# The feed-forward layer's gate and up projection with the weights as the stationary operand, and a down projection that starts before the last gate group is out

## What is computed

```python
h = rmsnorm(x, g_pre_ffn[l]) * (1.0 + sc_f) + sh_f
f = (jax.nn.silu(h @ w_gate[l]) * (h @ w_up[l])) @ w_down[l]
x = x + gt_f * rmsnorm(f, g_post_ffn[l])
```

## Time and profile before

| | |
|---|---|
| median of 3 runs | 2523.65 us (2519.93 to 2524.54) |
| the profiled execution, device time | 2519.91 us |
| its span, first to last instruction | 2518.1 us |
| mean granted TensorE clock | 0.978 of full speed (full is 2.4 GHz) |
| TensorE busy with matmuls | 2365.1 us, 94% of the span |
| VectorE, ScalarE, GpSimd busy | 66%, 45%, 4% |
| read from HBM | 596.74 MB, 238 GB/s over the span |

### The profile page before, as it was taken

One profiled execution on the slowest core, in us unless ns is written; L12 is line 12 of the kernel. 1 busy time (PEld: TensorE's weight loads), 2 busy tenths in 40 slices (PEclk: granted clock), 3 DMA queues, 4 the chain that ended last, 5 costly groups with the idle time before them and its releaser, 6 DMA issues.

```text
span 2518.1 us, 27287 instructions
## 1 busy us (share of the span) xinstructions
PE 2365.1 (94%) x10764; PEld 1956.9 (78%) x10764; DVE 1669.7 (66%) x1786; ACT 1133.4 (45%) x1473; POOL 98.1 (4%) x62
## 2 busy tenths in 40 slices
PE   1399999979999999899969999999999999999997
PEld 1288788868888888788858888888888888888886
DVE  6898778978888888655554555556556555555565
ACT  2244666554444444444454433443445544444453
POOL 1000000001111111200000000000000001000000
PEclk9599999989999999999989999999999999999999
DMA  8898668958899999755534655555655657655553
GB/s 324 342 353 321 210 223 311 344 207 325 325 327 326 331 325 328 281 203 196 188 130 162 210 182 189 181 180 177 209 199 198 207 197 247 212 186 198 184 188 113
DMA packets 246612, 600.51 MB, mean 238 GB/s; under 512 B 11800, under 2 KB 12120, under 8 KB 239968
## 3 DMA queue, kind: packets, MB, share of 16 engines
q1 hardware_dynamic: 243520, 589.43, 67.1%
q0 software_dynamic: 2976, 9.49, 1.2%
HBM read 596.74 MB, written 2.13 MB: 238 GB/s over the span
## 4 chain that ended last, share of the span: by engine, by line
PE 90%; DVE 6%; ACT 1%; DMA 1%; issue 1%; DVEq 0%; SPq 0%; ACTq 0%
PE PS L1151 19%; PE PS L1152 19%; PE PS L1157 19%; PE PS L1123 10%; PE PS L1126 10%; PE PS L1132 10%; DVE BIAS L1562 4%; DMA RAW<-in_w_ada 1%; DVE LO L1544 1%; PE PS L1477 1%; PE PS L1247 0%; PE PS L1222 0%; PE PS L1423 0%; PE PS L1140 0%; PE PS L1194 0%
## 5 line engine op out<-in xcount | busy, mean ns | idle before, releaser
L1544 DVE TENSOR_TENSOR LO<-RAW,HI 128x1024 fp32r<-128x1024 f32 x808 | 1014.4, 1260 | 740.1 <-ACT HI L657 738.9
L657 ACT ACTIVATE HI<-RAW 128x1024 fp32r<-128x1024 f32 x808 | 854.3, 1059 | 1230.0 <-PE PS L1157 732.4
L1151 PE MATMUL PS<-HI,XH 128*128 128x512 f32 x2176 | 863.3, 397 | 3.1 <-DVE XL L1693 3.1
L1152 PE MATMUL PS<-HI,XL 128*128 128x512 f32 x2176 | 849.2, 390 | 0.0
L1157 PE MATMUL PS<-LO,XH 128*128 128x512 f32 x2176 | 583.4, 390 | 0.0
L1151 PEld LDWEIGHTS PS<-HI,XH 128*128 128x128 f32 x2176 | 409.8, 188 | 92.1 <-ACT HI L657 4.3
L1157 PEld LDWEIGHTS PS<-LO,XH 128*128 128x128 f32 x2176 | 409.0, 188 | 86.1
L1152 PEld LDWEIGHTS PS<-HI,XL 128*128 128x128 f32 x2176 | 409.7, 188 | 82.5 <-issue 1.0
L1562 DVE SCALAR_TENSOR_TENSOR BIAS<-RAW,CACT,BIAS 128x1024 f32<-128x1024 f32 x270 | 346.3, 1283 | 19.0 <-DMA RAW<-in_w_ada 11.4
L1123 PE MATMUL PS<-HI,XH 128*128 128x512 f32 x1056 | 327.7, 392 | 4.1 <-ACT HI L657 4.0
L1126 PE MATMUL PS<-HI,XL 128*128 128x512 f32 x1056 | 326.0, 390 | 0.0
(11 more groups left out here) (283 smaller groups left out, 1016.1 us busy)
## 6 DMA issues: line engine op xcount, KB each, us to landing
RAW<-in_w_in SPq DMA_DIRECT2D x208, 1024.0 KB, 5.0
RAW<-in_w_ada SPq DMA_DIRECT2D x144, 1024.0 KB, 5.7
RAW<-in_w_gate SPq DMA_DIRECT2D x88, 512.0 KB, 4.6
RAW<-in_w_up SPq DMA_DIRECT2D x88, 512.0 KB, 5.7
RAW<-in_w_down SPq DMA_DIRECT2D x44, 1024.0 KB, 4.8
RAW<-in_w_out SPq DMA_DIRECT2D x32, 1024.0 KB, 5.2
RAW<-in_w_proj_b SPq DMA_DIRECT2D x16, 1024.0 KB, 5.1
RAW<-in_w_proj_a SPq DMA_DIRECT2D x16, 1024.0 KB, 5.1
```

What stands on the lines that cost most here:

```text
L657: act.activation(HI[:, (it["half"] + hf) % HLS, :], RAW[:, it["slot"], hf * 1024:(hf + 1) * 1024], ACT.Copy).then_inc(s.hi_ready, 1)
L1151: pe.matmul(PS[:, bank + u, :], XH[:, 2 * n + kk, rows], hi, start=start and kk == 0, stop=False)
L1152: pe.matmul(PS[:, bank + u, :], XL[:, 2 * n + kk, rows], hi, start=False, stop=False)
L1544: dve.tensor_tensor(LO[:, slot, :], RAW[:, it["slot"], hf * 1024:(hf + 1) * 1024], HI[:, slot, :].bitcast(F32), ALU.subtract).then_inc(s.l ...
```

## The change

The matmuls of gate and up swap their operands. `turned_products` uses as stationary operand 128 of the 1024 weight columns of a half and as moving operand all 256 positions of XH or XL: 8 blocks of columns, each with HI by XH and HI by XL, then 8 with LO by XH, 24 matmuls in all. Block j goes to bank `4q + j // 2`, columns 0 to 255 or 256 to 511, so the gate columns take banks 4q and 4q + 1, the up columns 4q + 2 and 4q + 3. Only the first matmul into a bank carries `start`. The results now have the inner features on the partitions: `gated` writes its product straight to `FT`, and `f_turn`, `f_chunks` and the semaphore `f_t` are gone; what waited for `group_out` waits for `f_ready`.

At the end of the layer the first down tile is worked off in two parts: both its weight halves for positions 128 to 255 (banks 4 to 7), then, after a wait for `f_ready` 11, both for positions 0 to 127 (banks 0 to 3, where group 10 lay). `group_evac(10)` and `gated(10)` move behind the first down halves on ACT and DVE, `root_table()` behind the eighth. `products` gets an argument `rows`, which positions it works on.

```diff
@@ -259,7 +259,7 @@
 
     add("ada", [("A",)] * 32, 1)
     add("first", first_body(), 1)
-    add("ffn", ffn_body(), 1, groups=11, per_slot_dmas=2)
+    add("ffn", ffn_body(), 1, per_slot_dmas=2)
     add("down", [("W", k) for k in range(4)], NKF // 4)
     add("second", [("W", g, k) for g in range(GROUPS_2) for k in range(0, NK, 4)], 1, groups=GROUPS_2)
     assert plan.ada == ADA_GROUPS
@@ -661,17 +661,9 @@
 
                 q, sec = g % 2, secs["ffn"]
                 act.wait_ge(s.half_used, sec.half(0, 16 * (g + 1)))
-                wait(act, s.f_t, g - 1)
-                act.activation(FG[:, q, :].rearrange("p (u n) -> p u n", u=NT),
-                               PS[:, 4 * q:4 * q + 4:2, :], ACT.Silu).then_inc(s.f_silu, 1)
-
-            def f_chunks(g):
-
-                q = g % 2
-                act.wait_ge(s.f_t, g + 1)
-                act.activation(FT[:, 4 * g:4 * g + 4, :],
-                               PS[:, 4 * q:4 * q + 2, :].rearrange("p b (k t) -> p (b k) t", t=S),
-                               ACT.Copy).then_inc(s.group_out, 1)
+                wait(act, s.f_ready, g - 1)
+                act.activation(FG[:, q, :].rearrange("p (b n) -> p b n", b=2), PS[:, 4 * q:4 * q + 2, :], ACT.Silu)\
+                   .then_inc(s.f_silu, 1)
 
             def stream(name):
                 sec = secs[name]
@@ -679,13 +671,21 @@
                 def emit(i):
                     first = isinstance(i, int) and i == 0
                     for it in sec.items:
-                        k = 4 * i + it["what"][0]
-
-                        act.wait_ge(s.half_used, sec.half0 if first else sec.half(i, it["half"]) - 6)
-                        act.activation(XH[:, it["what"][0], :], FT[:, bass.ds(k, 1), :].rearrange("p a t -> p (a t)"),
+                        kk = it["what"][0]
+                        k = 4 * i + kk
+                        if first:
+                            act.wait_ge(s.half_used, secs["ffn"].half(0, 160 + kk + 1))
+                        else:
+                            act.wait_ge(s.half_used, sec.half(i, it["half"]) - 6)
+                            act.wait_ge(s.f_ready, 11)
+                        act.activation(XH[:, kk, :], FT[:, bass.ds(k, 1), :].rearrange("p a t -> p (a t)"),
                                        ACT.Copy).then_inc(s.xs_hi, 1)
                         for hf in range(2):
+                            if first and kk == 1 and hf == 1:
+                                group_evac(10)
                             hi_half(sec, i, it, hf)
+                        if first and kk == 3:
+                            root_table()
                 looped(act, sec, emit)
 
             def squares(src_of, junk):
@@ -966,11 +966,7 @@
                     at = h % 16
                     if g and at == 3:
                         group_evac(g - 1)
-                    if g and at == 13:
-                        f_chunks(g - 1)
-            group_evac(10)
-            f_chunks(10)
-            root_table()
+            act.wait_ge(s.f_ready, 1)
             stream("down")
             post(3, secs["down"])
             row_norm(4, 2)
@@ -1112,34 +1108,34 @@
 
         @block.tensor
         def _(pe):
-            def products(ready, slot, slot_k, bank_of, first, last):
+            def products(ready, slot, slot_k, bank_of, first, last, rows=range(NT)):
 
                 pe.wait_ge(s.hi_ready, ready)
-                for u in range(NT):
-                    rows = slice(u * P, (u + 1) * P)
-                    xh, xl = XH[:, slot_k, rows], XL[:, slot_k, rows]
+                for u in rows:
+                    xh, xl = (v[:, slot_k, u * P:(u + 1) * P] for v in (XH, XL))
+                    for x in (xh, xl):
+                        for cc in range(2):
+                            pe.matmul(PS[:, bank_of(u, cc), :], x, HI[:, slot, cc * 512:(cc + 1) * 512],
+                                      start=first and x is xh, stop=False)
+                pe.wait_ge(s.lo_ready, ready)
+                for u in rows:
                     for cc in range(2):
-                        cols, o = slice(cc * 512, (cc + 1) * 512), PS[:, bank_of(u, cc), :]
-                        pe.matmul(o, xh, HI[:, slot, cols], start=first, stop=False)
-                    for cc in range(2):
-                        cols, o = slice(cc * 512, (cc + 1) * 512), PS[:, bank_of(u, cc), :]
-                        pe.matmul(o, xl, HI[:, slot, cols], start=False, stop=False)
+                        m = pe.matmul(PS[:, bank_of(u, cc), :], XH[:, slot_k, u * P:(u + 1) * P],
+                                      LO[:, slot, cc * 512:(cc + 1) * 512], start=False, stop=last)
+                return m
+
+            def turned_products(ready, slot, k, bank, first, last):
+
+                pe.wait_ge(s.hi_ready, ready)
+                for j in range(8):
+                    w, o = HI[:, slot, j * P:(j + 1) * P], PS[:, bank + j // 2, j % 2 * S:j % 2 * S + S]
+                    pe.matmul(o, w, XH[:, k, :], start=first and j % 2 == 0, stop=False, skip_group_check=True)
+                    pe.matmul(o, w, XL[:, k, :], start=False, stop=False, skip_group_check=True)
                 pe.wait_ge(s.lo_ready, ready)
-                for u in range(NT):
-                    rows = slice(u * P, (u + 1) * P)
-                    for cc in range(2):
-                        cols, o = slice(cc * 512, (cc + 1) * 512), PS[:, bank_of(u, cc), :]
-                        m = pe.matmul(o, XH[:, slot_k, rows], LO[:, slot, cols], start=False, stop=last)
+                for j in range(8):
+                    m = pe.matmul(PS[:, bank + j // 2, j % 2 * S:j % 2 * S + S], LO[:, slot, j * P:(j + 1) * P], XH[:, k, :],
+                                  start=False, stop=last, skip_group_check=True)
                 m.then_inc(s.half_used, 1)
-
-            def f_turn(g):
-                q = g % 2
-                pe.wait_ge(s.f_ready, g + 1)
-                for kk in range(4):
-                    for u in range(NT):
-                        m = pe.transpose(PS[:, 4 * q + kk // 2, (kk % 2) * S + u * P:(kk % 2) * S + (u + 1) * P],
-                                         FG[:, q, u * 512 + kk * P:u * 512 + (kk + 1) * P], IDENT[:])
-                m.then_inc(s.f_t, 1)
 
             def narrow(sec, h, n, bank, start, stop):
 
@@ -1165,11 +1161,20 @@
                     first = isinstance(i, int) and i == 0
                     for it in sec.items:
                         k = it["what"][0]
+                        pe.wait_ge(s.xs_lo, 4 * i + k + 1)
+                        if k == 0 and first:
+                            for rows in ((1,), (0,)):
+                                if rows == (0,):
+                                    pe.wait_ge(s.f_ready, 11)
+                                for hf in range(2):
+                                    m = products(sec.half(i, hf) + 1, hf, 0, lambda u, cc: 4 * u + 2 * hf + cc, True, False, rows)
+                                    if rows == (0,):
+                                        m.then_inc(s.half_used, 1)
+                            continue
                         for hf in range(2):
                             h = it["half"] + hf
-                            if hf == 0:
-                                pe.wait_ge(s.xs_lo, 4 * i + k + 1)
-                            products(sec.half(i, h) + 1, h % HLS, k, lambda u, cc: 4 * u + 2 * hf + cc, k == 0 and first, k == 3 and last_pass)
+                            products(sec.half(i, h) + 1, h % HLS, k, lambda u, cc: 4 * u + 2 * hf + cc, False, k == 3 and last_pass)\
+                                .then_inc(s.half_used, 1)
                 emit(0)
                 with pe.Fori(1, sec.n_iter - 1) as i:
                     emit(i)
@@ -1390,20 +1395,16 @@
                 for hf in range(2):
                     h = it["half"] + hf
                     if k + hf == 0:
-                        wait(pe, s.group_out, g - 1)
+                        wait(pe, s.f_ready, g - 1)
                     if h < 16 and h % 2 == 0:
                         pe.wait_ge(s.x_ready, TURNED[0] + h // 2 + 1)
-                    products(sec.half(0, h) + 1, h % HLS, k + hf, lambda u, cc: 4 * q + 2 * u + cc, k + hf == 0, k + hf == NK - 1)
+                    turned_products(sec.half(0, h) + 1, h % HLS, k + hf, 4 * q, k + hf == 0, k + hf == NK - 1)
                     if h in (1, 3, 5, 7):
                         turn_pair(0, 4 + h // 2)
-                    if k + hf == 9 and g:
-                        f_turn(g - 1)
                     if g == 10 and k + hf == 13:
                         pe.wait_ge(s.mod_in, 32)
                         pe.wait_ge(s.f_ready, 10)
                         pe.transpose(PS[:, 6, 0:64], MODT[:, :], IDENT[0:64, 0:64]).then_inc(s.mod_t, 1)
-            f_turn(10)
-            pe.wait_ge(s.group_out, 11)
             pe.wait_ge(s.mod_ready, 3)
             stream("down")
             pe.wait_ge(s.post_done, 4)
```

(9 more changed lines are left out.)

## The result

The changed kernel takes 2533.64 us (2531.73 to 2534.58, 6 runs), the kernel before 2522.46 us (2519.93 to 2525.92, 6 runs beside them). The ratio is 1.0043 with a 95% interval of 1.003 to 1.0056: 11.2 us slower. The profiled execution took 2531.75 us, its span is 2529.9 us at a mean clock of 0.979 (before: 2519.91, 2518.1, 0.978).

What follows compares the result with a forecast made beforehand. TensorE's own stream was taken as the bound; +4.9 (matmuls), -9.0 (transposes) and -7.65 (hole before down) gave 2508.2 us for the profiled execution, 2512 us against the median, with an 8-in-10 range of 2502 to 2537.

Steps and rivals of the forecast that it cites:

- What bounds the kernel: Whole kernel: TensorE's own stream sets the time, PE busy 94% of the span, 100 of 100 us inside gate and up.
- Part 1: Gate and up: 24 matmuls of 256 columns at 114.5 ns make a half 2.748 us, not 2.72; +4.9 us.
- half of the 10: Gate and up: of 10 ns lost while float32r columns stream, 256 columns lose 5, plus 3 per matmul; 114.7 ns.
- The prediction's own sign of being wrong: Gate and up: matmul pace outside 113 to 116 ns, or TensorE waiting there for `HI`, `LO` or weights.
- the toll: Gate and up: the 13.4 ns are a fixed loss per matmul, 120.1 ns at 256 columns; +28.6 us, chance 0.24.
- Part 2: Inside gate and up: ten groups' transposes, 0.9 us each, leave TensorE's stream; -9.0 us.
- Part 3: Step before down: early down matmuls shrink 9.35 us lost to a 1.7 us wait for VectorE; -7.65 us.
- The first rival: Gate and up: twice as many matmuls pay 13.4 ns each, +28.6 us in place of +4.9; 2535.6 us, chance 0.24.
- the second: Gate and up: weight loads decide the pace, 111 ns per matmul, -9.9 us; 2497 us, chance 0.12.
- The third: Step before down: VectorE held again or clock falling to 1.2 GHz, -2.1 in place of -7.65; 2517.5 us, chance 0.10.
- The fourth: Gate and up: no float32r pace at 256 columns, 217 ns per matmul, +437 us; 2944 us, chance 0.04.

Runs made afterwards that it cites:

- The chains: Kernels with the whole computation left out, running only 96 matmuls of each form back to back; float32r paces 226.7 ns at 512 columns, 120.0 at 256.
- The experiment with the old step: Changed kernel, but group 10 evacuated and the table loaded before the first down tile, which is worked off whole again: 2538.95 us, ratio 1.0061.

## Why the prediction was wrong

**What bounds the kernel: right.** TensorE's stream set the time in gate and up, nothing waited for `HI`, `LO` or weights, and the loads' own row, full for 100 of 100 us now, did not decide: the pace is 120.0 and a load's floor 111.7. The chains bear out that floor, which the prediction had read as 111 in the earlier trace rows.

**Part 1, the matmuls: wrong, and this is nearly the whole miss.** The step that failed is "I take half of the 10 for half the columns". The bound above it, "if the 13.4 ns are a fixed toll per matmul, 106.7 + 13.4 = 120.1 ns", is what happened: 120.0. So the term was +28.2 us (176 x 0.16) and not +4.9, 23.3 us more, of the 23.6 by which the profiled execution (2531.75) missed the forecast for it (2508.2). The prediction's own sign of being wrong, a pace outside 113 to 116 ns, was met. The evidence that led there was plain float32 at 256 columns, which streams as long as 512 columns of float32r and loses 10 ns less. The observation stands (215.8 beside 226.7 ns in the chains; by their count it is one of two records that a float32 matmul leaves, so the "two clocks per column" of the prediction are those of a record, not of a matmul), but it compares two types and says nothing of two widths. A comparison of types at one stream length can't divide a loss between columns and matmuls; only the same type at two widths can, and the trace held none. With one width known, the toll was the simpler reading of the earlier trace rows, and at 0.24 it was given too little. Even so it holds for this form and not as a law: with 64 stationary columns the loss does grow with the width, 6.7 ns at 256 and 16.7 at 512. That 2533.64 lies inside the range for 8 in 10, up to 2537, comes of stretching the range to this rival; the forecast itself had the wrong sign.

**Part 2, the transposes: right.** Gate and up grew by 18.85 us; with +28.2 for the matmuls, -9.35 is left, beside the -9.0 of 10 x 0.9. In the trace of before a half with the transposes behind it takes 3.515 us and the next one 2.82 to 2.83, against 2.720: 0.90 us for each.

**Part 3, the hole: right in mechanism, a little small.** -8.7 in place of -7.65. The wait came out at 0.65 us, not 1.7: VectorE was through with the modulation at 1057.67, 2.0 us ahead of 1059.65, where down can start (before 1037.79 and 1039.17, 1.4 us), about half of that because its addition began earlier, about half because it took 3.29 us and not 3.61; and its queue took 1057.70 to 1063.01, 5.31 us, not 5.72, because neighbouring operations overlap a little. The clock stayed at 1.00. The 0.17 us that were lost just behind the wait are not in these 0.65. The experiment with the old step shows the same from the other side: about 5 us of the 8.7 belong to the early start; the rest went with the last group's transposes, the chunks behind them and part of the wait.

**The sum.** With the measured terms it is 28.2 - 9.35 - 8.7 = 10.15; with 0.2 inside down, 1.63 ahead (not put down to the change) and -0.2 behind, that is the 11.8 of the profiled executions, and the medians say 11.2. The first rival's own number, 2535.6, is 2 us off: the -1.05 of part 3, and a median of before that came out 1.2 us lower over six runs. The measured pace, 120.0, also lies beyond the 117.3 ns per matmul above which the rival had the change come out slower.

**The other rivals.** The loads' 111.7 ns show only from some 224 columns down, so the second falls. The third (the hole stays in part) falls with 0.65 us. The fourth falls too: with 24 matmuls and 24 loads, 164 of the 176 halves took 2.88 us.

## What to carry to other kernels

Before swapping the operands of a product, count its matmuls: which side moves sets how many there are (256 positions moving make twice as many as 512 weight columns), and every one loses something beside its columns, 13.3 ns here for float32r with 128 stationary columns at 512, 384, 320 and 256, against 2.5 ns for bfloat16. A loss known at one width is to be priced as fixed per instruction too, and another type's row doesn't decide it; a chain of 96 matmuls of the very form does. And take a change apart: this one joined a loss of 19 us to a gain of 8.7, and the gain alone, put on the kernel before, gave 2515.41 us, below both.

## What the runs showed of the hardware beside this

- Plain float32 leaves two records for each matmul, 215.8 ns each at 256 moving columns and 429.2 at 512, 111.7 at 128. So a float32 matmul of 512 columns costs 858 ns, 3.8 times a float32r one.
- Fewer stationary columns can cost pace: 226.7 ns with 128, 233.3 with 120, 230.0 with 96 or 64, 231.7 with 32, all float32r with 512 moving.
- Two forms in turn are slower than their own paces add up to: bfloat16 beside float32r at 256 columns pays 15 ns a pair.
- VectorE's addition of 32 columns took 3.29 us beside POOL's reduction over the partitions, as the 3.61 in the earlier trace rows. Beside the seven other reductions of either trace a `LO` of 128x1024 took 4.0 to 5.6 us instead of 1.22. The Trainium skill, SBUF — State Buffer, section SBUF: two separate sides, calls the port pair of VectorE and GpSimd an exclusive lock, held for the whole instruction; it concerns a VectorE instruction with two SBUF inputs when GpSimd's reads SBUF. By that page the addition would end behind POOL's instruction. In the trace it ended at 1057.45 and POOL's row at 1058.99, and the next VectorE operations ran at 0.18, 0.42 and 2.35 us (for two) beside the rest of it. So the trace agrees in part: the hold is there, and it ended 1.5 us ahead of the row's end. The profile gives spans on POOL only roughly, so how much of the instruction it covers stays open.
